# Two-block transformer kernel: the first feed-forward multiplies chunks that lack the norm's root

## What is computed

```
def rmsnorm(x, g):
    y = xf * lax.rsqrt(jnp.mean(xf * xf, axis=-1, keepdims=True) + EPS)
    return (y * g)

def conv_glu(x, w_gate, w_up, conv_w, conv_b, w_down):     # D_FF = 5632
    g = x @ w_gate
    u = x @ w_up
    gp = jnp.pad(g, ((0, 0), (1, 1), (0, 0)))
    gc = conv_b
    for i in range(3):
        gc = gc + conv_w[i] * gp[:, i:i + L]
    return (jax.nn.silu(gc) * u) @ w_down
...
        h = h + mix @ w_out[l]
        h = h + conv_glu(rmsnorm(h, ffn_norm_g[l]), w_gate[l], w_up[l], conv_w[l], conv_b[l], w_down[l])
```

## Time and profile before

| | |
|---|---|
| median of 3 executions | 2664.8 us (2663.4 to 2665.21) |
| profiled execution, first to last instruction | 2665.4 us |
| TensorE busy | 2611.4 us (98%) |
| VectorE busy | 1842.1 us (69%) |
| ScalarE busy | 1248.7 us (47%) |
| GpSimd busy | 333.6 us (13%) |

### The profile page before, as it was taken

The page is one execution under the profiler, slowest core; times in us unless marked ns, Lnnn a source line. Parts: engine busy times, 40 slices in busy tenths (PEclk is TensorE's granted clock), DMA queues, the critical chain, the costliest instruction groups (busy, mean ns, idle before and its releaser), DMA issues.

```text
span 2665.4 us, 51392 instructions
## 1 busy us (share of the span) xinstructions
PE 2611.4 (98%) x22052; PEld 2581.0 (97%) x22052; DVE 1842.1 (69%) x2596; ACT 1248.7 (47%) x1943; POOL 333.6 (13%) x526
## 2 busy tenths in 40 slices
PE   7999999999999999999999999999999999999998
PEld 7898889999999999999999999999999999999998
DVE  6756578877777777787888667776877645454544
ACT  5556665544433444445434443334554443444443
POOL 2110101111121111231000001110211000000001
PEclk9999999999999999999999999999999999999999
DMA  6433455688898878886444578886768656655563
GB/s 207 139 116 100 120 161 174 195 269 270 268 296 282 278 268 269 273 293 212 146 156 157 181 233 284 277 283 221 256 216 277 222 187 196 199 193 190 189 190 128
DMA packets 500085, 571.22 MB, mean 214 GB/s; under 512 B 26705, under 2 KB 473425, under 8 KB 499857
## 3 DMA queue, kind: packets, MB, share of 16 engines
q1 hardware_dynamic: 467968, 463.76, 53.2%
q0 software_dynamic: 31600, 103.80, 12.1%
q10 hardware_dynamic: 288, 0.36, 0.0%
HBM read 565.77 MB, written 2.54 MB: 213 GB/s over the span
## 4 chain that ended last, share of the span: by engine, by line
PE 87%; DVE 7%; ACT 4%; issue 1%; DMA 0%; POOL 0%; SPq 0%; DVEq 0%; ACTq 0%
PE ps L730 27%; PE ps L732 27%; PE ps L731 27%; DVE wl L1841 3%; ACT wh L1329 1%; PE ps L1030 1%; PE ps L859 1%; PE ps L698 1%; PE ps L700 1%; PE ps L699 1%; DVE nx L1945 1%; DVE lr L2037 1%; DMA raw<-in_w_in 0%; PE ps L832 0%; PE ps L875 0%
## 5 line engine op out<-in xcount | busy, mean ns | idle before, releaser
L1841 DVE TENSOR_TENSOR wl<-raw,wh 128x1024 fp32r<-128x1024 f32 (+1 forms) x894 | 1057.5, 1199 | 553.7 <-ACT wh L1329 549.4
L1329 ACT ACTIVATE wh<-raw 128x1024 fp32r<-128x1024 f32 (+1 forms) x894 | 883.1, 1030 | 589.5 <-PE ps L732 573.8
L730 PE MATMUL ps<-xs,wh 128*128 128x256 f32 x2880 | 805.1, 280 | 5.3 <-DVE xs L1922 5.3
L731 PE MATMUL ps<-xs,wh 128*128 128x256 f32 x2880 | 798.6, 277 | 0.0
L732 PE MATMUL ps<-xs,wl 128*128 128x256 f32 x2880 | 798.5, 277 | 0.0
L730 PEld LDWEIGHTS ps<-xs,wh 128*128 128x128 f32 x2880 | 542.8, 188 | 7.0 <-DVE wl L1841 5.8
L731 PEld LDWEIGHTS ps<-xs,wh 128*128 128x128 f32 x2880 | 542.5, 188 | 1.0 <-issue 1.0
L732 PEld LDWEIGHTS ps<-xs,wl 128*128 128x128 f32 x2880 | 542.8, 188 | 0.0
L730 PE MATMUL ps<-hid,wh 128*128 128x256 f32 x1408 | 389.6, 277 | 0.0
L731 PE MATMUL ps<-hid,wh 128*128 128x256 f32 x1408 | 389.1, 276 | 0.0
L732 PE MATMUL ps<-hid,wl 128*128 128x256 f32 x1408 | 389.1, 276 | 0.0
(11 more groups left out here) (397 smaller groups left out, 3709.3 us busy)
## 6 DMA issues: line engine op xcount, KB each, us to landing
raw<-in_w_in SPq DMA_DIRECT2D x118, 1024.0 KB, 5.3
ada_raw<-in_w_ada POOLq DMA_DIRECT2D x384, 256.0 KB, 4.8
raw<-in_w_gate SPq DMA_DIRECT2D x44, 1024.0 KB, 6.2
raw<-in_w_up SPq DMA_DIRECT2D x44, 1024.0 KB, 7.0
raw<-in_w_ffn_gate SPq DMA_DIRECT2D x44, 1024.0 KB, 5.2
raw<-in_w_ffn_up SPq DMA_DIRECT2D x44, 1024.0 KB, 5.5
raw<-in_w_down SPq DMA_DIRECT2D x32, 1024.0 KB, 6.0
raw<-in_w_ffn_down SPq DMA_DIRECT2D x32, 1024.0 KB, 5.5
```

The lines of the kernel that those rows point to most:

```text
L730: pe.matmul(dst, h[:, c, o:o + w], moving(g, 0, k), start=(k == 0), stop=False)
L731: pe.matmul(dst, h[:, c, o:o + w], moving(g, 1, k), start=False, stop=False)
L1329: act.activation(wh[i % NS][:, part], raw[i % NR][:, part], ACT.Copy).then_inc(s_hi, 1)
L1841: dve.tensor_tensor(wl[i % NS][:, part], raw[i % NR][:, part], wh[i % NS][:, part].bitcast(F32), ALU.subtract).then_inc(s_lo, 1)
```

## The change

Gate and up products of the first feed-forward all read the chunks without the root; nothing is written a second time. The root is multiplied in when a gate bank is evicted, into `ssq_a` and `ssq_b` (`unscaled`, then for all 22 gates), and when a down bank is evicted (`scaled_residual`). The up bank stays unscaled, since the down product passes the missing factor on. Up products now read 258 positions, as gates do, since both take the same view. The chunks go directly to the 1280-byte homes, and the view of 258 positions starts where the 256 of the up did. The homes overlap the old operand of "outa", so that product's operand moves to homes of the same kind, `xa`. The squares are summed in chunk 8 of up 0 and no more of gate 0.

```diff
-    ffn(1, "w_gate", "w_up", "w_down", (XF, Q0, T), (XF, META, T))
+    ffn(1, "w_gate", "w_up", "w_down", (XF, Q0, T), (XF, Q0, T))
...
-RAW_T0 = {N_IN: Q0, N_FFN1: Q0, N_MIX2: 0, N_FFN2: 0}
-RAW_T1 = {N_IN: T, N_FFN1: T, N_MIX2: T - Q0, N_FFN2: T - Q0}
+RAW_T0 = {N_IN: Q0, N_FFN1: 0, N_MIX2: 0, N_FFN2: 0}
+RAW_T1 = {N_IN: T, N_FFN1: T - Q0, N_MIX2: T - Q0, N_FFN2: T - Q0}
...
         def slot(h, c):
             i = KD * h + c
             x, o = (xf_near, i * SLOT) if i < SLOTS else (xf_far, (i - SLOTS) * SLOT)
-            o += 48 * min(c, 1)
-            return x[:, o:o + T]
+            o += 64 if c else 16
+            return x[:, o:o + T - Q0]
+
+        def head_slot(h, c):
+            o = (8 * h + c) * SLOT + (64 if c else 16)
+            return xa[:, o:o + T - Q0]
...
+            def raw_ready(k):
+                pe.wait_ge(s_rl, raw_base(N_FFN1) + k + 1)
+
+            def sums_within(k):
+                if k == SUMS_AT[N_FFN1]:
+                    square_sums(N_FFN1)
...
+                        if b == 1:
+                            first = f == 0 and g == 0
+                            gemm((b, "gate", f, g), raw_ready if first else None)
+                            gemm((b, "up", f, g), sums_within if first else None)
...
+            def root_within(n):
+                yield from pause(ROOT_AT[n])
+                root(n)
...
-            lanes.start("norm", norm_his(N_FFN1, done(("outa", 7))), front=True)
+            lanes.start("norm", root_within(N_FFN1), front=True)
...
+            def reciprocal_within(n):
+                yield from pause(ROOT_AT[n])
+                reciprocal(n)
...
+            def scaled_residual(key, j, c, i):
+                s, _ = last_use(key, j)
+                x = ssq["ab"[j]][:, 0:SEQ]
+                if i >= 2:
+                    dve.wait_ge(s_dn, i - 1)
+                dve.tensor_tensor(x, ps[GEMMS[key].banks[j]][:, 0:SEQ], rstd[:, META - Q0:T - Q0], ALU.mult).then_inc(s, 1)
+                dve.wait_ge(*last_use(key, j))
+                dve.tensor_tensor(H[:, c, META:T], x, H[:, c, META:T], ALU.add).then_inc(s_dn, 1)
...
-            lanes.start("norm", norm_scales(N_FFN1), front=True)
+            lanes.start("norm", reciprocal_within(N_FFN1), front=True)
```

More of the change, by code:

```diff
@@ L155, in make_plan @@
             add(("na", p, n), "w_in", 0, 16, 1024 * n + 256 * p, 256, X0, Q0 if n == 0 else 0, T)
-    for n, k0, x in (("outb", 8, XB), ("outa", 0, X0)):
+    for n, k0, x in (("outb", 8, XB), ("outa", 0, XA)):
         for g in range(8):
@@ L396, in build @@
         assert off <= mla_end
+        xa, off = at("xa", [P, 16 * SLOT + 2], F32R, row_home(mla_end, wh_off - 64))
+        assert off <= limit
         raw_in, _ = at("raw_in", [P, 2, KD, T], F32R, limit // 32 * 32 - 8 * KD * T)
@@ L970, in ffn @@
                         n = N_FFN1 if b == 1 else N_FFN2
-                        if f == 0 and g == 0:
-                            if b == 2:
-                                lanes.stop("ada")
+                        if b == 1:
+                            first = f == 0 and g == 0
+                            gemm((b, "gate", f, g), raw_ready if first else None)
+                            gemm((b, "up", f, g), sums_within if first else None)
+                            if f == 0 and g == 1:
+                                lanes.start("ada", ada(), slow=True)
+                        elif f == 0 and g == 0:
+                            lanes.stop("ada")
                             gemm_raw(n, (b, "gate", f, g), square_sums)
@@ L978, in ffn @@
                             gemm((b, "up", f, g), normed(n))
[L979 to L982, removed]
+                            lanes.resume("ada")
                         else:
@@ L1654, in silu @@
                             for j in range(2):
[L1655 to L1658, removed]
+                                act.wait_ge(s_ft, first_use + j + 1)
                                 gc = gct[(first_use + j) % NGC]
@@ L2250, in ffn @@
                                 n = HALF * f + 2 * g + j
[L2251 to L2254, removed]
+                                gc, src, s = gct[u % NGC], ssq["ab"[j]], s_ft
                                 dve.wait_ge(s_gca, u + 1)
@@ L2298, in ffn @@
                             c = 2 * g + j
+                            if b == 1:
+                                scaled_residual((b, "down", f, g), j, c, KD * f + c)
+                                continue
                             if f == 1:
                                 dve.wait_ge(*last_use((b, "down", 0, g), j))
[L2301 removed]
+                            residual((b, "down", f, g), j, c, 16, mod[:, 80 + c:81 + c])
                         if b == 1 and f == 1 and g == 0:
```

48 lines of the change are left out of this document (24 added, 24 removed).

## The result

The changed kernel takes 2674.16 us (median of 13 runs, 2670.48 to 2677.65); the kernel before took 2666.27 us on the same chip (13 runs, 2663.4 to 2670.44). The ratio on record is 1.0025, 95% interval 1.0018 to 1.0032, so the change costs 6.7 us (4.8 to 8.5); the two medians differ by 7.9. It is a small loss, a quarter of a per cent, but the whole interval lies above 1. The forecast was +7.0.

The account below looks back on a forecast made before the run. The prediction took TensorE, 98% busy, as the bound, so matmul pace and its waits decide. Its terms summed to +7.0 us, which on 2664.8 us gives 2671.8 us, with a range of 2648 to 2683.

Parts of the forecast that it names:

- 21 ups other than up 1: First feed-forward ups: each goes from 11.13 to 11.56 us at 258 positions, +9.0 us in all.
- gate 2 and nineteen gates: First feed-forward gates: nineteen go from 11.52 to 11.56 us, +0.8; gate 2 loses its slow clock, -0.1.
- gates 0 and 1: First feed-forward's first gates: from 11.45 us without sums to the new pace, +0.2 us.
- outa: Eight products of 48 matmuls, 5.73 us each, go to half of 11.56 us: +0.4 us.
- The pace of 258 positions at the new home: First feed-forward gates and ups: 11.56 us a product, the middle of two near rows, bounds 11.02 and 11.84; chance 0.42.
- Rival 1: The new home gives 258 positions the good pace, 11.02 us a product: -18.9 us, 2645.9 us; chance 0.23.
- Rival 2: Only width counts: gates stay at 11.52 us, ups pay 0.08 each; -2.3 us, 2662.5 us; chance 0.12.
- rival 3: The new home is bad for 258 positions: 11.84 us a product, 13.4 us more, 2685 us; chance 0.23.
- The second writing goes: At up 1, writing chunks once removes TensorE's wait and slow clock: 16.62 us falls to 11.56, -5.1 us.
- The root comes later: Around up 0, ScalarE and VectorE hold at the root; TensorE waits 0.6 and 1.2 us, together +1.8 us.
- Evictions: Gates and downs: two more VectorE instructions each, hidden beside TensorE, so 0; up to 31 us if cover were gone.
- A rule against the rows: TensorE matmuls: the skill's isolated gap gives 109.2 ns for 256 positions; every row is above it.

Follow-up runs that it names:

- wide: The kernel before, with only the first feed-forward's ups widened to 258 positions, read from the gates' old place; ratio 1.0035 to the kernel before.
- up256: The changed kernel with first feed-forward ups back at 256 positions in their old place and gates starting 8 bytes lower; ratio 0.9981 to the kernel before.
- map: The kernel before, with second feed-forward gates and ups reading shifted and wider views, so it computes other numbers; ran once, 2690.35 us.
- sums0: The changed kernel with the three sums of squares moved back from up 0 to gate 0; ratio 1.0015 to the kernel before.
- both: The changed kernel with ups of 256 positions at their old place and the sums of squares back in gate 0; 2658.14 us, 0.9964 of the kernel before.
- evict2: The changed kernel with every eviction multiply by the root done twice on VectorE; ratio 1.0026 to the kernel before.
- kick: `both` with the first matmul of each first feed-forward up issued twice; ratio 0.9974 to the kernel before.

## Why the prediction was right

Each term as the two traces have it, before against after:

| term | predicted | in the trace |
|---|---|---|
| 21 ups other than up 1 | +9.0 | +9.1: +8.7 in the 20, +0.4 in up 0 without sums and waits |
| up 1 | -5.1 | -5.1 |
| gate 2 and nineteen gates | +0.7 | +0.5 |
| gates 0 and 1 | +0.2 | +0.3 |
| outa | +0.4 | +0.3 |
| root later | +1.8 | +1.9 |
| evictions | 0 | 0 |
| downs | none | +0.9 |
| sum | +7.0 | +7.9, and +8.1 for the stretch |

*The pace of 258 positions at the new home* was the term that decided, and it lies between the two neighbouring rows, 11.52 and 11.60: it is 11.53, and for gates behind an up with transposes 11.6 to 11.7. That the change loses the good pace is a matter of width, as `wide` and `up256` show. *Rival 1* came true at no start tried. *Rival 2* (width counts, at 0.83 ns) undersized it: 11.53 - 11.13 us over 96 matmuls is 4.2 ns.

That the value fell so close was in part luck. The middle of two rows is not a mechanism, and the rows spoke more for *rival 3* than the prediction saw. It calls chunk 4 of the earlier trace rows the only 258-wide chunk at the new start. But rows 1088 bytes apart come back to a start every fourth chunk, and chunks 8 and 9 of the same product repeat chunks 4 and 5:

```profile
1940.56:1941.30 0.74, 0.74 (x9) 1.00 0.00 0
1941.30:1942.02 0.72, 0.72 (x9) 1.00 0.00 0
```

So a quarter of the chunks showed 0.74 us at that start, and whole products from it take 11.64 to 11.76 us in `map`. At 11.76 the 48 lengths would have made the change 11 us dearer than it was; at the best home of `map`, 11.43, 5 us cheaper. The start modulo 256 bytes is thus not all of the home, and why rows 1280 bytes apart escape the slower pace no run shows.

*The second writing goes* was right in mechanism and size: up 1 is 11.53 with clock 1.00. *The root comes later* was right too, wait by wait, and `sums0` takes exactly these waits away. *Evictions* at nothing was right: `both` has them and its ups and downs are as short as before, and `evict2` shows it with twice the work. VectorE's work in the window of gate 3 and up 3 grew from 18.10 us to 18.87.

What the sum left out are the downs. It costed them by VectorE alone and took their pace as fixed. In both halves down 0 falls to 117.8 ns a matmul at its transposes and keeps that to its end (15.91 against 15.56 us), and down 1 begins so (15.12 against 15.00). Twice 0.47 us is 0.9. In the measured 6.7 it is hidden by the spread. The slow downs 0 go with the 258-wide ups at the new home and once, in `kick`, with 256-wide ones; the cause is open.

*A rule against the rows.* The measured gap at 258 positions is 120.1 ns; N / 2.4 + 2.5 ns, which the Trainium skill gives for an isolated matmul ("TensorE: Matmul & The Clock Gate", section "Back-to-back issue gap"), would be 110.0. These streams do not come down to it at either width: 256 positions range from 113.6 to 120.0 ns (10.91 and 11.52 us for 96) by the start alone, which the formula has no term for. So the home does matter, to both widths.

What stays open: why 256 positions at that one start reach 113.3 ns, why 258 positions from the same start are slower in rows of 1024 bytes than in rows of 1280, and what sets the pace of a down at its transposes.

## What to carry to other kernels

Before a matmul is made "a little wider" to share a view, look for two products of the trace that differ by just that width, and take the price from their windows, not from the added columns: here 2 of 258 columns cost 3.6% of each up. If the home changes too, look at every chunk that shares the new start, not at one. A removed wait of 5 us is one event and a slower pace is paid 22 times, so count the repeats first. And when work moves to an eviction, move the sums that it depends on no later than they were: the queues of two engines hold at the root. `both`, which leaves the ups at 256 positions and the sums where they were, keeps the gain without the price.

## What the runs showed of the hardware

- 256 positions have two paces at one home, 113.3 and 117.8 ns a matmul (10.93 and 11.31 us for 96, with a first dozen at about 118 in both). Behind a 258-wide gate they mostly alternate from up to up in `both`, and one extra matmul at the start put every up into the good one. Four transposes can switch a product in its middle, to the good pace (up 2 of the second half before, 11.44 us) or to the slow one (down 0 of the changed kernel). A pace is kept across products: a slow down 0 hands it to the first matmuls of down 1 (15.12 against 15.00 us).
- At 258 the home moves the pace from 119.1 to 122.5 ns (11.43 to 11.76 us), and the start modulo 256 bytes does not fix it: one start takes 11.53 in rows of 1280 bytes and 11.64 to 11.76 in rows of 1024. 260 positions at that start take 120.3 ns, 272 at 248 bytes 126.7.
- VectorE had room for 76 multiplies more beside this TensorE stream (19.60 us of work in 23.06); 805 us became 0.7 longer, 0.5 of it in the one product where VectorE was late already.
